# Stick-breaking attention by pairs of heads, with filler products and early output chunks

## Chip, cores and metric

One core of a Trainium2 chip runs the whole program. Its engines are TensorE (matrix products), VectorE, ScalarE and GpSimd, with SyncE for issuing transfers; each takes its own instructions in order and they meet through semaphores. The metric is the device time of one execution in microseconds (us).

## The reference

The program runs two transformer-like blocks of two layers each on 256 tokens of 1024 features, in float32. Only one sublayer bears on the change: stick-breaking attention, in the first layer of the second block, 16 heads of 64.

```python
def stick_breaking_attention(h, w_qkv, w_o):
    ...
    q = qkv[0] * (SB_HEAD_DIM ** -0.5)
    k, v = qkv[1], qkv[2]
    for blk in range(S // Q_BLOCK):
        ...
        z = jnp.einsum('bhqd,bhkd->bhqk', q[:, :, t0:L], k[:, :, :L])
        mask = s_idx[None, :] < t_idx[:, None]
        log_keep = jnp.where(mask, jax.nn.log_sigmoid(-z), 0.0)
        later = lax.cumsum(log_keep, axis=3, reverse=True) - log_keep
        w = jnp.where(mask, jnp.exp(jax.nn.log_sigmoid(z) + later), 0.0)
        outs.append(jnp.einsum('bhqk,bhkd->bhqd', w, v[:, :, :L]))
    ...
    return o @ w_o
```

With sp(z) = log(1 + e^z), which is -log_keep, a weight is exp(z - the sum of sp over this key and all later ones), and zero where the mask is off.

## The kernel before

The program is a list of stages (`plan`). Most are slab stages: a weight slab of 16 blocks of 128 x 128 arrives in `raw`, ScalarE rounds it to `w_hi` (L633), VectorE subtracts the rest into `w_lo` (L1166), and TensorE multiplies it with three products per block (`mm3`, L1911 to L1913: high by high, high by low, low by high). A slab has two halves f of 8 chunks k; slabs alternate between two places p. Beside them VectorE makes modulation products (L1194) from rows that GpSimd's queue loads.

The stage `stick` stands between the projections for q, k and v (L825 is the last copy of v) and the output projection (`out`, kind "b"). Keys lie on the partitions. A head has 384 columns of scores: 256 queries for the first 128 keys and 128 queries for the last 128 keys. For each head h, by step:

- TensorE: scores z into `pb[0][:, h % 2]` (L2315, L2316, float32, over 64 rows).
- ScalarE: w = ln(1 + exp(-|z|)) in three chained instructions (L1055 to L1057), read from PSUM.
- VectorE: zm = z + mask (0 or -1e30, L1792), w = max(z, 0) + w, which is sp(z) (L1794), and w times the 0/1 mask on the two outer thirds (L1797).
- TensorE, for head h - 2: products of w with a triangular table and with a table of -1, which give the negative sums over this and later keys, into `pb[1]` (L2324 to L2327).
- VectorE, for head h - 1: adds zm to them (L1801). ScalarE, for head h - 2: exp (L1061).
- TensorE, for head h - 4: products with v into half of the rows of `ps_o` (L2337 to L2339). ScalarE and VectorE then make the high and low part of the result in `e_hi`, `e_lo` (L1066, L1807).

`sb_z` in the arena has three turns of three 384-column buffers. In step h == 3 VectorE also makes the last two modulation products of the stage before. The output projection's first half slab waits for the low parts chunk by chunk (in `half`), f = 0 for all k, then f = 1.

Of the kernel before, what the change touches and what calls it, by code (L numbers as in the profile page):

```python
# [25 lines left out]
P = 128  # L26
# [50 lines left out]
TB = T + 2  # L77

# [67 lines left out]
def build(nc, a):  # L146
# [148 lines left out]
    with ExitStack() as ctx:  # L295
# [60 lines left out]
        sb_z = view(6144, 3, 3, 384)  # L356
# [5 lines left out]
        assert free0 + 4096 <= 11392 and 8320 + 2 * RC * P <= 11392 and 6144 + 3456 <= 11392  # L362
# [55 lines left out]
        def table(name):  # L418
# [37 lines left out]
        st_z, st_ln, st_sp, st_r, st_v, st_w, st_o, st_hi, st_lo = (  # L456
            sem(f"st_{k}") for k in ("z", "ln", "sp", "r", "v", "w", "o", "hi", "lo"))
# [158 lines left out]
        def _(act):  # L616
# [431 lines left out]
            def do_stick(n):  # L1048
                for h in range(SB_H + 4):
                    if h < SB_H:  # L1050
                        act.wait_ge(st_z, h + 1)
                        z, w = pb[0][:, h % 2, 0:384], sb_z[:, h % 3, 0, :]

                        wait_up(act, st_r, h - 2)
                        link(nc.scalar.activation(w, z, ACT.Abs))  # L1055
                        link(nc.scalar.activation(w, w, ACT.Exp, scale=-1.0))
                        nc.scalar.activation(w, w, ACT.Ln, bias=1.0).then_inc(st_ln, 1)  # L1057
                    if 2 <= h < SB_H + 2:
                        k = h - 2
                        act.wait_ge(st_v, k + 1)  # L1060
                        nc.scalar.activation(sb_z[:, k % 3, 2, :], sb_z[:, k % 3, 1, :], ACT.Exp).then_inc(st_w, 1)  # L1061
                    if h >= 4:
                        k = h - 4
                        r = HD * (k % 2)
                        act.wait_ge(st_o, k + 1)
                        nc.scalar.activation(e_hi[r:r + HD, k // 2, :], ps_o[r:r + HD, k % 2, 0:T],  # L1066
                                             ACT.Copy).then_inc(st_hi, 1)
# [81 lines left out]
        def _(dve):  # L1149
# [632 lines left out]
            def do_stick(n):  # L1782
                edges = lambda v: v.rearrange("p (b c) -> p b c", b=3)[:, 0:3:2, :]
                sv = next(s for what, s in plan if what == "slabs" and s.kind == "v" and s.arg["heads"] == SB_H)
                dve.wait_ge(masks_in, 16)
                for h in range(SB_H + 4):
                    if h < SB_H:
                        z, w, zm = pb[0][:, h % 2, 0:384], sb_z[:, h % 3, 0, :], sb_z[:, h % 3, 1, :]
                        dve.wait_ge(st_ln, h + 1)

                        wait_up(dve, st_w, h - 2)
                        nc.vector.tensor_tensor(zm, z, masks[:, 384:768], ALU.add).then_inc(st_sp, 1)  # L1792

                        nc.vector.scalar_tensor_tensor(out=w, in0=z, scalar=0.0, in1=w, op0=ALU.max, op1=ALU.add)\  # L1794
                            .then_inc(st_sp, 1)
                        dve.wait_ge(st_sp, 3 * h + 2)
                        nc.vector.tensor_tensor(edges(w), edges(w), edges(masks[:, 0:384]), ALU.mult).then_inc(st_sp, 1)  # L1797
                    if 1 <= h <= SB_H:
                        k = h - 1
                        dve.wait_ge(st_r, k + 1)  # L1800
                        nc.vector.tensor_tensor(sb_z[:, k % 3, 1, :], pb[1][:, k % 2, 0:384], sb_z[:, k % 3, 1, :],  # L1801
                                                ALU.add).then_inc(st_v, 1)
                    if h >= 4:
                        k = h - 4
                        r = HD * (k % 2)
                        dve.wait_ge(st_hi, k + 1)
                        nc.vector.tensor_tensor(e_lo[r:r + HD, k // 2, :], ps_o[r:r + HD, k % 2, 0:T],  # L1807
                                                e_hi[r:r + HD, k // 2, :].bitcast(F32), ALU.subtract)\
                            .then_inc(st_lo, 1)
                    if h == 3:  # L1810
                        mods(sv, sv.bodies - 1, 1, False, True)
# [92 lines left out]
        def _(pe):  # L1904
# [123 lines left out]
            def half(s, b, p, f, is_first):  # L2028
# [17 lines left out]
                else:  # L2046
                    xs = chunks(s, b, p, f)
                    n, one = len(xs), s.kind == "down"
                    for k, x in enumerate(xs):
                        if is_first and p == 0 and f == 0:  # L2050
# [3 lines left out]
                            if s.kind == "out" and s.arg["kind"] == "b":  # L2054

                                pe.wait_ge(st_lo, 2 * k + 2)
# [89 lines left out]

            def open_pair(i):
# [9 lines left out]
            def do_slabs(s):  # L2157
                def body(b, is_first, last):
                    for p in range(2):
# [14 lines left out]
                        elif s.kind == "merge" and is_first and p == 0:  # L2174
                            merge_first(s)
                        else:
# [127 lines left out]

            def do_stick(n):
                pe.wait_ge(tab_in, 16)
                pe.wait_ge(q_copied, n["had"]["q"])
                pe.wait_ge(v_copied, n["had"]["v"])
                for h in range(SB_H + 4):
                    if h < SB_H:  # L2310

                        wait_up(pe, st_sp, 3 * h - 4)
                        c, r = h // 2, HD * (h % 2)
                        q, k_ = dst["sbq"][r:r + HD, c, :], dst["sbk"][r:r + HD, c, :]
                        nc.tensor.matmul(pb[0][:, h % 2, 0:256], k_[:, 0:P], q, start=True, stop=True)  # L2315
                        nc.tensor.matmul(pb[0][:, h % 2, 256:384], k_[:, P:T], q[:, P:T], start=True, stop=True)\  # L2316
                            .then_inc(st_z, 1)
                    if 2 <= h < SB_H + 2:
# [192 lines left out]
```

## Time and profile before

| | |
|---|---|
| median of 3 runs | 2317.43 us (2315.99 to 2321.75) |
| span of the profiled execution | 2318.1 us |
| TensorE products busy | 2228.3 us (96%) |
| VectorE, ScalarE busy | 1837.1 us (79%), 1308.9 us (56%) |
| stick stage, first scores to first output product | 1546.2 to 1597.9 us |
| mean granted TensorE clock | 0.984 |

The profile is of one execution. Busy times of an engine are shares of that span; a wait is shown as idle time in front of an instruction with what released it. The granted clock is 1.00 at 2.4 GHz and 0.50 at 1.2 GHz.

### The profile page before, as it was taken

The page shows a single profiled execution, that of the slowest core. Times are in us where ns is not written, and L with a number is a line of the kernel's source. Part 1 is how long each engine was busy: PE and PEld are TensorE (multiplying, and loading weights), DVE is VectorE, ACT ScalarE, POOL GpSimd, SP SyncE. Part 2 cuts the span into 40 slices and gives each one's busy share as a digit, 9 for nine tenths or more (in the row PEclk, how much of TensorE's full clock was granted, in tenths as well). Part 3 has the DMA queues.
Part 4 walks back from the last instruction along what each step waited for, and adds up shares of the span by engine and source line. Part 5 has one row for each costly group of instructions (what it writes and reads, how often), then busy time and mean ns, then how long its engine had stood idle before and what let it go on. Part 6 is the DMA issues. An engine that isn't in the chain of part 4 may idle for free.

```text
span 2318.1 us, 49499 instructions
## 1 busy us (share of the span) xinstructions
PE 2228.3 (96%) x18082; PEld 2145.7 (93%) x18082; DVE 1837.1 (79%) x3245; ACT 1308.9 (56%) x2142; POOL 119.9 (5%) x231
## 2 busy tenths in 40 slices
PE   7899999999999999999999999999999999979998
PEld 5798899998899999889999999988999999979998
DVE  4886866799789988978998878768877877878655
ACT  4366655536776554576665644657544644686443
POOL 0100000000000100000000001010001001000000
PEclk8999999999999999999999999999999999999999
DMA  9745676765358765534778687662777677635654
GB/s 360 243 143 188 231 243 203 257 200 172 116 172 276 266 229 199 174 119 163 241 261 281 230 272 265 212 224 82 236 276 264 227 278 267 229 118 178 227 168 132
DMA packets 150550, 499.80 MB, mean 216 GB/s; under 512 B 17408, under 2 KB 21632, under 8 KB 148864
## 3 DMA queue, kind: packets, MB, share of 16 engines
q1 hardware_dynamic: 113504, 374.01, 47.0%
q0 software_dynamic: 32544, 119.55, 16.3%
q10 hardware_dynamic: 4352, 4.20, 0.6%
q8 instruction: 99, 1.62, 0.3%
q14 instruction: 51, 0.42, 0.1%
HBM read 496.65 MB, written 1.05 MB: 215 GB/s over the span
## 4 chain that ended last, share of the span: by engine, by line
PE 71%; DVE 15%; ACT 6%; DMA 4%; issue 3%; ACTq 0%; SPq 0%; DVEq 0%; POOLq 0%; POOL 0%
PE bank_pair L1911 22%; PE bank_pair L1913 21%; PE bank_pair L1912 21%; DVE w_lo L1166 4%; DVE arena L1452 2%; DMA modraw<-in_w_mod 2%; ACT w_hi L633 2%; PE bank_pair L2034 1%; PE ps_o L1924 1%; DVE h_lo L1328 1%; DVE small L1528 1%; ACT arena L873 1%; DVE arena L1725 1%; ACT h_hi L718 1%; DMA e_plain<-in_w_mod 0%
## 5 line engine op out<-in xcount | busy, mean ns | idle before, releaser
L1166 DVE TENSOR_TENSOR w_lo<-raw,w_hi 128x1024 fp32r<-128x1024 f32 (+2 forms) x748 | 820.9, 1113 | 198.9 <-ACT w_hi L633 195.1
L633 ACT ACTIVATE w_hi<-raw 128x1024 fp32r<-128x1024 f32 (+2 forms) x748 | 714.2, 967 | 406.8 <-PE bank_pair L1913 274.3
L1911 PE MATMUL bank_pair<-h_hi,w_hi 128*128 128x256 f32 x2928 | 841.8, 287 | 13.3 <-DVE arena L1725 5.8
L1912 PE MATMUL bank_pair<-h_lo,w_hi 128*128 128x256 f32 x2928 | 831.4, 284 | 0.0
L1913 PE MATMUL bank_pair<-h_hi,w_lo 128*128 128x256 f32 x2928 | 831.3, 284 | 0.0
L1911 PE MATMUL bank_pair<-e_both,w_hi 128*128 128x256 f32 (+1 forms) x2064 | 593.0, 287 | 19.0 <-DVE e_both L1846 10.0
L1911 PEld LDWEIGHTS bank_pair<-h_hi,w_hi 128*128 128x128 f32 x2928 | 564.8, 193 | 35.5 <-issue 25.0
L1912 PE MATMUL bank_pair<-e_both,w_hi 128*128 128x256 f32 (+1 forms) x2064 | 587.4, 285 | 0.0
L1913 PE MATMUL bank_pair<-e_both,w_lo 128*128 128x256 f32 (+1 forms) x2064 | 587.2, 285 | 0.0
L1912 PEld LDWEIGHTS bank_pair<-h_lo,w_hi 128*128 128x128 f32 x2928 | 565.1, 193 | 0.3
L1913 PEld LDWEIGHTS bank_pair<-h_hi,w_lo 128*128 128x128 f32 x2928 | 564.8, 193 | 0.0
L1911 PEld LDWEIGHTS bank_pair<-e_both,w_hi 128*128 128x128 f32 x2064 | 399.0, 193 | 26.9 <-issue 16.7
L1912 PEld LDWEIGHTS bank_pair<-e_both,w_hi 128*128 128x128 f32 x2064 | 399.4, 194 | 0.3
L1913 PEld LDWEIGHTS bank_pair<-e_both,w_lo 128*128 128x128 f32 x2064 | 399.1, 193 | 0.0
L1194 DVE SCALAR_TENSOR_TENSOR modraw<-modraw,cact 128x1024 f32<-128x1024 f32 x174 | 211.9, 1218 | 20.2 <-DMA modraw<-in_w_mod 19.8
L588 POOL DMA_DIRECT2D modraw<-in_w_mod x216 | 114.1, 529 | 1997.7 <-DVE modraw L1194 1657.9
L1452 DVE SCALAR_TENSOR_TENSOR arena<-arena,par 128x256 f32<-128x256 f32 x360 | 149.8, 478 | 4.0 <-PE bank_pair L2254 3.8
L1725 DVE SCALAR_TENSOR_TENSOR arena<-bank_pair,par,arena 128x255 f32<-128x255 f32 x240 | 99.3, 477 | 40.1 <-ACT arena L1007 39.0
L1038 ACT ACTIVATE arena<-bank_pair 128x256 f32<-128x256 f32 x80 | 30.7, 383 | 114.2 <-PE bank_pair L1913 114.2
L1005 ACT ACTIVATE arena<-bank_pair,par 128x256 f32<-128x256 f32 x60 | 33.8, 564 | 104.1 <-PE bank_pair L1913 104.1
L1634 DVE SCALAR_TENSOR_TENSOR x_res<-bank_pair,cols,x_res 128x256 f32<-128x256 f32 (+1 forms) x128 | 60.6, 481 | 27.2 <-PE bank_pair L1913 25.8
L1760 DVE TENSOR_TENSOR arena<-bank_pair,arena 128x256 f32<-128x256 f32 x80 | 33.9, 424 | 48.7 <-ACT arena L1038 48.7
(264 smaller groups left out, 2176.2 us busy)
## 6 DMA issues: line engine op xcount, KB each, us to landing
modraw<-in_w_mod POOLq DMA_DIRECT2D x216, 512.0 KB, 4.9
raw<-in_w_gu SPq DMA_DIRECT2D x176, 512.0 KB, 4.6
raw<-in_w_up SPq DMA_DIRECT2D x132, 512.0 KB, 5.1
raw<-in_w_gate SPq DMA_DIRECT2D x48, 512.0 KB, 3.7
raw<-in_w_dn SPq DMA_DIRECT2D x64, 384.0 KB, 4.3
raw<-in_w_dn SPq DMA_DIRECT2D x64, 320.0 KB, 3.5
raw<-in_w_down SPq DMA_DIRECT2D x48, 384.0 KB, 5.0
raw<-in_w_down SPq DMA_DIRECT2D x48, 320.0 KB, 4.4
```

The lines of the kernel that those rows point to most:

```text
L588: nc.gpsimd.dma_start(modraw[:, c, :], a["w_mod"][m, :, D * c:D * (c + 1)]).then_inc(mod_in[c], 16)
L633: nc.scalar.activation(w_hi[:, p, HALF * f:HALF * f + w], raw[:, p, HALF * f:HALF * f + w], ACT.Copy)\
L1005: nc.scalar.activation(scr[:, p, 0, :], z[:, 0, :], ACT.Identity, bias=fb[:, j, :], scale=taps[:, j, 1:2])
L1166: nc.vector.tensor_tensor(w_lo[:, p, at], raw[:, p, HALF * f:HALF * f + w], w_hi[:, p, at].bitcast(F32), ALU.subtract).then_inc(lo_ready, 1)
L1194: nc.vector.scalar_tensor_tensor(out=modraw[:, p, :], in0=modraw[:, p, :], scalar=1.0, in1=vector, op0=ALU.mult, op1=ALU.mult, accum_out=m ...
L1452: ins = nc.vector.scalar_tensor_tensor(out=o, in0=u, scalar=w[:, j, t:t + 1], in1=o, op0=ALU.mult, op1=ALU.add)
L1634: nc.vector.scalar_tensor_tensor(out=x[:, k, :], in0=pb[p][:, q, 0:T], scalar=cols[:, 2, :].unsqueeze(2)[:, k, :], in1=x[:, k, :], op0=ALU ...
L1725: nc.vector.scalar_tensor_tensor(out=o, in0=i_, scalar=taps[:, FC * q + j, 0:1] if left else taps[:, FC * q + j, 2:3], in1=o, op0=ALU.mult ...
L1760: ins = nc.vector.tensor_tensor(scr[:, p, 1, :], z[:, 1, 0:T], scr[:, p, 0, :], ALU.mult)
L1911: nc.tensor.matmul(out, l[0], r[0], start=start, stop=False)
L1912: nc.tensor.matmul(out, l[0], r[1], start=False, stop=False)
L1913: return nc.tensor.matmul(out, l[1], r[0], start=False, stop=stop)
```

## The change

Two heads (a pair, i = 0 to 7) are handled together.

- Each VectorE and ScalarE operation covers 2 x 384 columns. `sb_z` has three turns of two buffers of 768 columns; the closing exp writes over the first.
- The mask is added first, by VectorE from PSUM; ScalarE's abs, exp and ln then read the masked scores from the arena, and the multiplication with the 0/1 mask is gone. The tri-products take all 384 columns of a head in one product, and a second one adds the later keys' sums.
- Products of the two heads alternate: scores on rows 0 to 63 and 64 to 127, values on columns 0 to 63 and 64 to 127 of the array.
- In step i TensorE makes the scores of pair i, the tri-products of i - 1 and the values of i - 2. VectorE: mask addition i, max-and-add i - 1, addition i - 2, low part i - 3. ScalarE: abs, exp, ln of i, copy of i - 3, closing exp of i - 2.
- `keep_warm` adds 3 and 6 float32 products of 256 columns, whose results nobody reads, after the scores of pairs 0 and 1.
- Ahead of the values of the last pair TensorE makes chunks 0 to 4 of both halves of the first output slab (`out_early`); chunks 5 to 7 follow (`out_rest`), in the order k, f.
- The two modulation products go to step 9, between the last addition and the low part of pair 6.

```diff
             def do_stick(n):                         # ScalarE
+                for i in range(SB_P + 3):
+                    if i < SB_P:
+                        w, zm = sb_z[:, i % 3, 0], sb_z[:, i % 3, 1]
+                        act.wait_ge(st_zm, i + 1)
+                        wait_up(act, st_o, i - 2)
+                        link(nc.scalar.activation(w, zm, ACT.Abs))
                         link(nc.scalar.activation(w, w, ACT.Exp, scale=-1.0))
                         nc.scalar.activation(w, w, ACT.Ln, bias=1.0).then_inc(st_ln, 1)
+                    if i >= 3:
+                        k = i - 3
+                        act.wait_ge(st_o, k + 1)
+                        nc.scalar.activation(e_hi[:, k, :], ps_o[:, k % 2, 0:T], ACT.Copy).then_inc(st_hi, 1)
+                    if 2 <= i < SB_P + 2:
+                        k = i - 2
                         act.wait_ge(st_v, k + 1)
+                        nc.scalar.activation(sb_z[:, k % 3, 0], sb_z[:, k % 3, 1], ACT.Exp).then_inc(st_w, 1)
...
             def do_stick(n):                         # VectorE
+                for i in range(SB_P + 3):
+                    if i < SB_P:
+                        dve.wait_ge(st_z, i + 1)
+                        wait_up(dve, st_w, i - 2)
+                        nc.vector.tensor_tensor(sb_z[:, i % 3, 1], pb[0][:, :, 0:384], far, ALU.add).then_inc(st_zm, 1)
+                    if 1 <= i < SB_P + 1:
+                        k = i - 1
+                        w, zm = sb_z[:, k % 3, 0], sb_z[:, k % 3, 1]
+                        dve.wait_ge(st_ln, k + 1)
+                        nc.vector.scalar_tensor_tensor(out=w, in0=zm, scalar=0.0, in1=w, op0=ALU.max, op1=ALU.add)\
                             .then_inc(st_sp, 1)
+                    if 2 <= i < SB_P + 2:
+                        k = i - 2
                         dve.wait_ge(st_r, k + 1)
+                        nc.vector.tensor_tensor(sb_z[:, k % 3, 1], pb[1][:, :, 0:384], sb_z[:, k % 3, 1],
                                                 ALU.add).then_inc(st_v, 1)
+                    if i == SB_P + 1:
+                        mods(sv, sv.bodies - 1, 1, False, True)
+                    if i >= 3:
+                        k = i - 3
                         dve.wait_ge(st_hi, k + 1)
+                        nc.vector.tensor_tensor(e_lo[:, k, :], ps_o[:, k % 2, 0:T], e_hi[:, k, :].bitcast(F32),
+                                                ALU.subtract).then_inc(st_lo, 1)
...
+            def out_chunk(f, k):
+                pe.wait_ge(st_lo, k + 1)
+                c = HALF * f + P * k
+                return mm3(pb[0][:, f, 0:T], (w_hi[:, 0, c:c + P], w_lo[:, 0, c:c + P]),
+                           (e_hi[:, k, :], e_lo[:, k, :]), k == 0, k == DC - 1)
+            def out_early(s):
+                pe.wait_ge(lo_ready, 2 * s.l0 + 2)
+                pe.wait_ge(st_zm, SB_P)
+                for f in range(2):
+                    for k in range(SBO_EARLY):
+                        out_chunk(f, k)
+            def out_rest(s):
+                for k in range(SBO_EARLY, DC):
+                    for f in range(2):
+                        ins = out_chunk(f, k)
+                        if k == DC - 1:
+                            ins.then_inc(half_done, 1)
...
+            def keep_warm(n):
+                for _ in range(n):
+                    nc.tensor.matmul(ps_t[:, 0, 0:T], ones, table("cos"), start=True, stop=True)
...
             def do_stick(n):                         # TensorE
+                for i in range(SB_P + 2):
+                    if i < SB_P:
+                        wait_up(pe, st_zm, i)
+                        for keys, queries, at in ((slice(0, P), slice(0, T), slice(0, T)),
+                                                  (slice(P, T), slice(P, T), slice(T, T + P))):
+                            for hd in range(2):
+                                r = HD * hd
+                                ins = nc.tensor.matmul(pb[0][:, hd, at], dst["sbk"][r:r + HD, i, keys],
+                                                       dst["sbq"][r:r + HD, i, queries], start=True, stop=True)
+                        ins.then_inc(st_z, 1)
+                        if i < len(ST_WARM):
+                            keep_warm(ST_WARM[i])
+                    if 1 <= i < SB_P + 1:
+                        k = i - 1
+                        pe.wait_ge(st_sp, k + 1)
+                        wait_up(pe, st_v, k)
+                        for hd in range(2):
+                            w, o = sb_z[:, k % 3, 0, hd], pb[1][:, hd, :]
+                            nc.tensor.matmul(o[:, 0:384], table("ntri"), w, start=True, stop=False)
+                            ins = nc.tensor.matmul(o[:, P:T], table("nones"), w[:, T:T + P], start=False, stop=True)
+                        ins.then_inc(st_r, 1)
+                    if i >= 2:
+                        k = i - 2
+                        if k == SB_P - 1:
+                            out_early(so)
                         pe.wait_ge(st_w, k + 1)
                         wait_up(pe, st_lo, k - 1)
+                        for keys, queries, at in ((0, slice(0, T), slice(0, T)), (1, slice(T, T + P), slice(P, T))):
+                            for hd in range(2):
+                                v = dst["sbv"][:, keys, HD * (2 * k + hd):HD * (2 * k + hd + 1)]
+                                ins = nc.tensor.matmul(ps_o[HD * hd:HD * (hd + 1), k % 2, at], v,
+                                                       sb_z[:, k % 3, 0, hd, queries], start=keys == 0, stop=keys == 1)
+                        ins.then_inc(st_o, 1)
```

SB_P is 8 (pairs), SBO_EARLY is 5, ST_WARM is (3, 6).

## Rows read from the trace of the kernel before

**Rows 1.** The page's first line.
```profile
span 2318.1 us, 49499 instructions
```

**Rows 2.** Stretches: length, busy us of PE, PEld, DVE, ACT, POOL; clock, DMA, GB/s.
```profile
1547.13:1550.51 3.38, 0.00 (x0) 0.00 (x1) 3.35 (x7) 2.96 (x6) 0.53 (x1) 1.00 1.00 372
1551.30:1561.50 10.20, 10.20 (x39) 8.62 (x38) 5.63 (x13) 5.90 (x12) 0.00 (x0) 0.50 0.25 86
1561.60:1595.90 34.30, 34.12 (x229) 28.13 (x227) 30.35 (x66) 27.76 (x60) 1.05 (x2) 1.00 0.10 32
```

**Rows 3.** Time order of PE over one head: start us, us, engine, line, operands.
```profile
1586.41 0.70 PE L2315 MATMUL bank_pair<-arena 64*128 64x256 f32 x2
...
1587.26 0.49 PE L2324 MATMUL bank_pair<-arena,tab 128*128 128x128 f32 x2
...
1588.35 0.43 PE L2337 MATMUL ps_o<-arena 128*64 128x128 f32 x2
...
1589.14 0.48 PE L2315 MATMUL bank_pair<-arena 64*128 64x256 f32 x1
```

**Rows 4.** Time order of PE, one head's scores at half clock.
```profile
1553.39 1.22 PE L2315 MATMUL bank_pair<-arena 64*128 64x256 f32 x2
...
1554.97 0.79 PE L2324 MATMUL bank_pair<-arena,tab 128*128 128x128 f32 x2
```

**Rows 5.** Time order of PE in the first block's attention, scores of two heads.
```profile
983.62 1.13 PE L2254 MATMUL bank_pair<-arena 64*128 64x256 f32 x8
984.68 0.39 PE L1911 MATMUL bank_pair<-h_hi,w_hi 128*128 128x256 f32 x1
```

**Rows 6.** Time order: first scores and their reader; later, ScalarE's sequence.
```profile
1546.17 0.34 PEld L2315 LDWEIGHTS bank_pair<-arena 64*128 64x128 f32 x4 [0.95 <-issue]
...
1547.12 0.49 ACT L1055 ACTIVATE arena<-bank_pair 128x384 f32<-128x384 f32 x1 [1.07 <-PE bank_pair L2316]
...
1587.89 0.52 ACT L1056 ACTIVATE arena<-arena 128x384 f32<-128x384 f32 x1
...
1588.44 0.52 ACT L1057 ACTIVATE arena<-arena 128x384 f32<-128x384 f32 x1
...
1589.04 0.52 ACT L1061 ACTIVATE arena<-arena 128x384 f32<-128x384 f32 x1
...
1589.47 0.36 ACT L1066 ACTIVATE e_both<-ps_o 64x256 fp32r<-64x256 f32 x1
```

**Rows 7.** Groups of instructions by form: count, busy us, mean ns, idle before.
```profile
L1166 DVE TENSOR_TENSOR w_lo<-raw,w_hi 128x768 fp32r<-128x768 f32 x112 | 104.8, 955 | 23.4 <-ACT w_hi L633 23.1
L633 ACT ACTIVATE w_hi<-raw 128x768 fp32r<-128x768 f32 x112 | 93.5, 844 | 117.1 <-PE bank_pair L1913 63.8 <-DMA raw<-in_w_down 39.8 <-DMA raw<-in_w_dn 12.9
L1066 ACT ACTIVATE e_both<-ps_o 64x256 fp32r<-64x256 f32 x13 | 4.8, 371 | 0.3
L1194 DVE SCALAR_TENSOR_TENSOR modraw<-modraw,cact 128x1024 f32<-128x1024 f32 x174 | 211.9, 1218 | 20.2 <-DMA modraw<-in_w_mod 19.8
```

**Rows 8.** Time order of DVE, its first instruction in the stage.
```profile
1549.44 0.55 DVE L1792 TENSOR_TENSOR arena<-bank_pair,bias 128x384 f32<-128x384 f32 x1
```

**Rows 9.** Stretches of TensorE waits and of what came after two of them.
```profile
184.73:187.08 2.35, 0.00 (x1) 0.01 (x1) 2.25 (x7) 2.34 (x4) 0.00 (x0) 1.00 0.01 5
189.40:192.70 3.30, 3.30 (x18) 3.30 (x17) 1.33 (x4) 3.19 (x7) 0.00 (x0) 0.50 0.02 5
...
1293.61:1295.07 1.46, 0.00 (x1) 0.03 (x1) 1.33 (x2) 1.46 (x3) 0.00 (x0) 1.00 0.00 0
1295.10:1302.00 6.90, 6.83 (x55) 6.62 (x56) 6.90 (x14) 3.74 (x6) 0.00 (x0) 1.00 0.53 173
```

**Rows 10.** Time order of PE, the first output products.
```profile
1597.86 0.39 PE L1911 MATMUL bank_pair<-e_both,w_hi 128*128 128x256 f32 x1
...
1598.32 0.28 PE L1911 MATMUL bank_pair<-e_both,w_hi 128*128 128x256 f32 x1
...
1598.67 0.28 PE L1911 MATMUL bank_pair<-e_both,w_hi 128*128 128x256 f32 x1
```

More of the change, by code:

```diff
@@ L77 @@
 TB = T + 2
+SB_P = SB_H // 2
+SBO_EARLY = 5
+ST_WARM = (3, 6)
 F32 = mybir.dt.float32
@@ L361, in build @@
         l_i, l_t = e_plain[:, 0, RC:2 * RC, :], e_plain[:, 1, RC:2 * RC, :]
-        assert free0 + 4096 <= 11392 and 8320 + 2 * RC * P <= 11392 and 6144 + 3456 <= 11392
+        assert free0 + 4096 <= 11392 and 8320 + 2 * RC * P <= 11392 and 6144 + 4608 <= 11392
         mod_first = [e_plain[:, e, DC * k:DC * (k + 1), :].rearrange("p a b -> p (a b)")
@@ L1782, in do_stick @@
             def do_stick(n):
-                edges = lambda v: v.rearrange("p (b c) -> p b c", b=3)[:, 0:3:2, :]
                 sv = next(s for what, s in plan if what == "slabs" and s.kind == "v" and s.arg["heads"] == SB_H)
+                far = masks[:, 384:768].unsqueeze(1).broadcast_to([P, 2, 384])
                 dve.wait_ge(masks_in, 16)
[L1786 to L1794, printed above, removed]
+                for i in range(SB_P + 3):
[8 more added lines that the diff above has]
+                        nc.vector.scalar_tensor_tensor(out=w, in0=zm, scalar=0.0, in1=w, op0=ALU.max, op1=ALU.add)\
@@ L2175, in body @@
                             merge_first(s)
+                        elif s.kind == "out" and s.arg["kind"] == "b" and is_first and p == 0:
+                            out_rest(s)
                         else:
@@ L2303, in do_gate @@
                         ins.then_inc(att_o, 1)
+            def keep_warm(n):
+                for _ in range(n):
+                    nc.tensor.matmul(ps_t[:, 0, 0:T], ones, table("cos"), start=True, stop=True)
             def do_stick(n):
+                so = next(s for what, s in plan if what == "slabs" and s.kind == "out" and s.arg["kind"] == "b")
                 pe.wait_ge(tab_in, 16)
@@ L2308, in do_stick @@
                 pe.wait_ge(v_copied, n["had"]["v"])
[L2309 to L2318, printed above, removed]
-                        k = h - 2
-                        pe.wait_ge(st_sp, 3 * (k + 1))
-                        wait_up(pe, st_v, k - 1)
-                        w, o = sb_z[:, k % 3, 0, :], pb[1][:, k % 2, :]
-                        nc.tensor.matmul(o[:, 256:384], table("ntri"), w[:, 256:384], start=True, stop=True)
-                        nc.tensor.matmul(o[:, 0:128], table("ntri"), w[:, 0:128], start=True, stop=True)
-                        nc.tensor.matmul(o[:, 128:256], table("ntri"), w[:, 128:256], start=True, stop=False)
-                        nc.tensor.matmul(o[:, 128:256], table("nones"), w[:, 256:384], start=False, stop=True)\
-                            .then_inc(st_r, 1)
-                    if h >= 4:
-                        k = h - 4
-                        r = HD * (k % 2)
```

43 lines of the change are left out of this document (3 added, 40 removed).

## The prediction

> **What bounds the kernel now.** I read the page first, then a table of stretches around the stick-breaking stage, then the time order of each engine inside it. The stage and the first half slab of the output projection are all that the diff touches: from the first score product at 1546.2 to the output products that start at 1597.86 [rows 10]. Everything before runs as it did; what follows runs later or earlier as a block. So the question is only when the first output slab's p = 0 is finished. Its 48 products follow each other every 0.12 us (a chunk of L1911 to L1913 each) [rows 10], 5.76 us, so it is finished at 1603.6.
>
> Inside the stage TensorE is the bound. In the long middle it is busy 34.12 of 34.30 us at full clock, VectorE 30.35 and ScalarE 27.76 [rows 2]. One head takes from 1586.41 to 1589.14, 2.73 us, and the three groups of products stand back to back: scores 0.85, tri-products (L2324 on) 1.09, values 0.79 [rows 3]. At the start there is a hole: TensorE waits 3.38 us after the first two heads' scores [rows 2] because VectorE is still with weight splits and begins the first mask addition at 1549.44 [rows 8]; after it the granted clock is 0.50 (1.2 GHz) for 10.2 us, although TensorE is busy all of it [rows 2]. A group then lasts about twice as long: one head's scores 1.58 [rows 4].
>
> **Part by part.** *Columns.* A product of 256 columns in this type costs two passes of 0.213 us. A group costs its passes plus 0.2 us: the value group, 6 passes of 128 columns, took 0.79 [rows 3]. The total of columns of a pair is that of two heads. What changes is that neighbouring products of scores now use different halves of the array's rows, and those of values different halves of its columns. The attention of the first block does that already: eight passes of L2254 (four products of 256 columns) stand from 983.62 to 984.68, 1.06 us, where one after another they would need 1.71 plus 0.2 [rows 5]. So they run two at a time. A pair's scores cost 0.43 + 0.21 + 0.2 = 0.84 us and its values 0.79, where two heads took 1.69 and 1.58; the tri-products cost 1.71 + 0.2 = 1.91, where they took 2.18. TensorE's work for a pair falls from 5.46 to 3.54 us.
>
> *VectorE and ScalarE.* The 768-wide form costs 0.955 us on VectorE and 0.844 on ScalarE [rows 7]. For a pair VectorE has three of them and a low part, 3.3 us (before, eight passes, two edge masks and two low parts, over 4.8); ScalarE has four and a copy, 3.8. No engine's sum would hold the stage above 3.9 us for a pair, against 5.46 now. By the sums it gets faster.
>
> *The order.* The sums don't decide, because three things that were two steps apart are now one. In step i ScalarE does abs, exp and ln of pair i, then the copy of i-3, then the closing exp of pair i-2. TensorE puts the values of pair i-2, which wait for that exp, ahead of the scores of pair i+1, which feed the mask addition and with it ScalarE's next step. Before, the values in a step were those of four heads back, whose exp had been made two steps earlier, so nothing closed. Now it is a ring, with every link in it:
> abs and exp 2 x (0.844 + 0.03) = 1.75 [rows 7], where the 0.03 is what lies between 1587.89 and 1588.44 beyond 0.52 [rows 6]; ln, next instruction 0.09 before its end as L1066 after L1061 [rows 6], 0.75; copy 0.38 - 0.09 = 0.29 (the one head's copy took 0.371 [rows 7]); closing exp 0.844 and 0.04 of handing over, 0.88; values 0.79; scores from first weight load to the reader's start 0.95, as from 1546.17 to 1547.12 [rows 6]; mask addition 0.955 + 0.04 = 0.99. Sum 6.40 us for a pair, against 2 x 2.73 = 5.46. The tri-products lie beside it: they wait for the two VectorE operations of 0.87 each that follow the mask addition, start 1.73 after ScalarE's step and end 3.64 after it, and the closing exp ends 3.68 after it. So they are hidden with nothing to spare.
>
> *The start.* Mask addition of pair 0 at 1549.44 as before [rows 8], to 1550.4; ScalarE 1550.4 to 1553.0 (before, it had worked from PSUM ahead of VectorE, and now has to wait). Scores 1 at 1550.4, added by 1552.3; ScalarE on pair 1 to 1555.5; the max-and-add of pair 0 ends 1554.0, tri-products 0 to 1555.9; scores 2, addition to 1557.85. ScalarE's step of pair 2 begins at 1557.9. The fillers, 9 products of 0.43 us, fill 1547.0 to 1548.3 and 1551.3 to 1553.9, in front of nothing that is ready; at full clock they cost nothing. Should the clock be low there, six of them take 5.1 us instead of 2.6 in front of the first tri-products and cost about 3 us.
>
> *The middle and the end.* Five rings later, step 7 begins at 1557.9 + 5 x 6.40 = 1589.9. Then tri-products 6 done at 1593.6; their addition, behind the max-and-add of pair 7, to 1594.9; tri-products 7 1594.9 to 1596.9; values 6 to 1597.6. Output chunks 0 to 4 for both halves, 30 products of 0.12 = 3.6 us, to 1601.3: the closing exp of pair 7 is ready at 1598.9, so the early chunks hold up its values by 2.4 us, but they are work that has to be done. Values 7 to 1602.1; chunks 5 and 6 (1.44 us) cover copy and low part of pair 7 (0.38 + 0.43, done 1603.2); chunk 7 to 1604.4. The two modulation products (1.218 us each [rows 7]), moved from the middle to this end, delay the low part of pair 6 to 1600.7, needed at 1602.2: cost nothing; with less cover at most 2.4 us. POOL's next load of modulation rows starts some 35 us later with them, into a queue that is idle here; the next such product belongs to the next feed-forward block. SP's queue isn't touched: the weight slabs of the output were loaded before. The later splits wait for TensorE's half slab 0, which now ends together with half 1, 2.9 us later in the slab; a copy of 1.05 and a subtraction of 1.22 fit into the 5.76 us of p = 1.
> End of p = 0: 1604.4 against 1603.6, +0.8 us at full clock. The gain of the start (its 10.2 us at 1.2 GHz) and of the covered end is eaten by 0.94 us for each ring.
>
> *The clock.* In the ring TensorE works 3.54 us on end and then waits 2.86 us (some 2.6 by the profile's modelled ends). What do such waits do in this trace? After one of 2.35 us (184.73) the clock was 0.50 for the whole of 189.4 to 192.7; after one of 1.46 us (1293.61) it stayed at 1.00 [rows 9]; the one of 3.38 us was followed by 10.2 us at 0.50 [rows 2]. The trace has ten waits of TensorE of 1.9 us and more, these two among them, and each was followed by a fall; of seven between 1.2 and 1.7 us at most two were. Here one comes every 6.4 us and the only fillers are in the first two steps. A ring wholly at 1.2 GHz costs: values 1.48 and scores 1.74 instead of 0.79 and 0.95, +1.5, and the tri-products 3.7 instead of 1.91, which then end 1.77 after the closing exp, +1.8: 9.65 us, +3.25. Bounds: no ring hit, 0; all six hit, +19.5. After a fall the clock stayed low at least 3.3 us [rows 9], which is about the busy half of one ring, and the next wait may or may not be in full after it has risen; I take half of the rings, 3 x 3.25 = +9.8.
>
> The Trainium skill, "TensorE: Matmul & The Clock Gate", section "Why this matters for your kernels", warns only of idle gaps longer than the ring's wait. By that rule alone the clock would hold and the sum would be +0.8; this trace disagrees, with the fall after 2.35 us.
>
> **The sum.** +0.8 + 9.8 = +10.6 us. The profiled span is 2318.1 [rows 1], 0.7 above the median 2317.4 of three runs; the difference is set against the median: 2328.0 us.
>
> **Rivals.**
> 1. *Ring at full clock.* As above, but the waits, which here stand between stretches of full work, don't lower the clock: +0.8, between -1 and +4 (4 with a slow start that the fillers lengthen): 2318.2. For it: after 1.46 us the clock held. Against: the wait of 2.35 us [rows 9] is the nearer one to 2.6. It is also what the rule of the Trainium skill's "TensorE: Matmul & The Clock Gate" gives.
> 2. *Low clock in all rings.* +0.8 + 19.5: 2337.7. For it: the 10.2 us at 0.50 under full work in just this stage [rows 2]. Against: in a slowed ring TensorE works 6.9 of 9.65 us on end, and the 3.3 us at full work [rows 9] sufficed for a rise.
> 3. *Faster.* ScalarE's own sum bounds and the ring does not close: 3.85 for a pair. Its place is the values of pair i-2 ahead of scores i+1; were they an operation that is already released when TensorE comes to it, step 7 would begin at 1577.1 and p = 0 end 12.8 us earlier than with the ring: 2317.4 + 0.8 - 12.8 = 2305.4. It decides for faster by 0.3% once a ring is below 4.8 us. Against: each link is a semaphore in the diff; only shorter durations could do it, and the 768 forms are measured [rows 7].
>
> **Chances.** Forecast (cost of the clock 6 to 14 us, 2324.3 to 2332.3) 0.58; rival 1 0.24; rival 2 and what lies above the forecast 0.09; rival 3 0.09. The range has to take in the forecast and rival 1, 0.82: 2316.5 to 2335. A difference of 0.3%, 7 us, is about what a measurement can tell from none. Slower by more: the forecast but for its lowest corner and rival 2, 0.65; within: rival 1 and that corner, 0.26; faster 0.09.
>
> **What would show it.** In the profile after: the starts of the abs operations 6.4 us apart where the clock is 1.00 and up to 9.7 where it is 0.50; the closing exp of pair i-2 right after the copy that follows ln; TensorE idle some 2.6 us before each tri-group, released by VectorE's addition; two heads' scores within 0.84 us; several stretches at 0.50 between 1557 and 1600; output chunks 0 to 4 ahead of the last values without a wait. I am wrong if abs operations are under 5.5 us apart (a link is missing from the ring) or PEclk stays at 1.00 through the stage (rival 1).

## The result and the profile after

| | before | after |
|---|---|---|
| median | 2318.1 us (10 runs, 2314.3 to 2323.3) | 2325.4 us (10 runs, 2320.6 to 2333.2) |
| ratio | | 1.0027, 95% interval 1.0016 to 1.0039 |
| the same on another chip | 2318.6 us (9 runs) | 2328.5 us (5 runs), 1.0041 (1.0027 to 1.0055) |
| span of the profiled execution | 2318.1 us | 2324.5 us |
| stage, first scores to end of first output slab | 57.5 us | 67.1 us |

The change makes the kernel slower, by 6.3 us by the ratio. The forecast was 10.6 us.

The page of the changed kernel, its first line and the busy times:

```profile
span 2324.5 us, 49225 instructions
...
PE 2219.3 (95%) x18004; PEld 2130.5 (92%) x18004; DVE 1823.2 (78%) x3197; ACT 1298.5 (56%) x2102; POOL 119.9 (5%) x231
```

TensorE, VectorE and ScalarE all do less than before (2219.3 against 2228.3 us on TensorE), and the kernel takes longer. The page can't show more: a slice is 58 us, about the whole stage. The stretches from one abs operation to the next show it; columns as in rows 2. The first line is the start (scores 0 to step 2), the next five are one ring each, the last goes from step 7 to the end of the output slab:

```profile
1542.67:1553.69 11.02, 8.89 (x50) 6.64 (x50) 6.36 (x9) 4.95 (x6) 0.53 (x1) 1.00 0.62 226
1553.69:1562.97 9.28, 6.39 (x24) 3.95 (x24) 2.69 (x4) 3.26 (x5) 0.00 (x0) 0.63 0.00 0
1562.97:1571.14 8.17, 5.29 (x24) 3.43 (x24) 3.12 (x5) 3.53 (x6) 0.00 (x0) 0.79 0.01 2
1571.14:1577.65 6.51, 3.63 (x24) 2.45 (x24) 3.11 (x5) 3.53 (x6) 0.00 (x0) 1.00 0.00 0
1577.65:1586.90 9.25, 6.36 (x24) 3.94 (x24) 3.11 (x5) 3.53 (x6) 0.00 (x0) 0.63 0.00 1
1586.90:1595.05 8.15, 5.27 (x24) 3.41 (x24) 3.11 (x5) 3.53 (x6) 0.00 (x0) 0.79 0.00 0
1595.05:1609.79 14.74, 12.31 (x89) 9.93 (x89) 9.05 (x15) 7.31 (x12) 1.06 (x2) 1.00 0.21 63
```

Where TensorE was busy 34.12 of 34.30 us [rows 2], it is now busy 3.63 of 6.51, and VectorE and ScalarE about half of the time: no engine is the bound. The ring at full clock takes 6.51 us; with the same 12 products in it (24 passes, x24) it takes up to 9.28 where the mean clock is 0.63.

The ring itself, in the time order of ScalarE over that clean stretch (start, duration, line; idle time and releaser in brackets):

```profile
1571.14 0.84 ACT L1058 ACTIVATE arena<-arena 128x768 f32<-128x768 f32 x1 [4.57 <-DVE arena L1793]
1572.01 0.84 ACT L1059 ACTIVATE arena<-arena 128x768 f32<-128x768 f32 x1
1572.89 0.84 ACT L1060 ACTIVATE arena<-arena 128x768 f32<-128x768 f32 x1
1573.64 0.36 ACT L1064 ACTIVATE e_both<-ps_o 128x256 fp32r<-128x256 f32 x1
1573.90 0.83 ACT L1069 ACTIVATE arena<-arena 128x768 f32<-128x768 f32 x1
1577.65 0.84 ACT L1058 ACTIVATE arena<-arena 128x768 f32<-128x768 f32 x1 [2.92 <-DVE arena L1793]
```

The time order of TensorE beside it (L2357 and L2358 tri-products, L2370 values, L2345 scores):

```profile
1572.98 0.89 PE L2357 MATMUL bank_pair<-arena,tab 128*128 128x384 f32 x2 [2.88 <-DVE arena L1803]
...
1574.57 0.39 PE L2358 MATMUL bank_pair<-arena,tab 128*128 128x128 f32 x2
1574.88 0.87 PE L2370 MATMUL ps_o<-arena 128*64 128x256 f32 x8
1575.68 0.92 PE L2345 MATMUL bank_pair<-arena 64*128 64x256 f32 x8
1579.49 1.62 PE L2357 MATMUL bank_pair<-arena,tab 128*128 128x384 f32 x2 [2.88 <-DVE arena L1803]
```

And VectorE's mask addition (L1793), max-and-add (L1798), addition (L1803) and the next mask addition:

```profile
1570.14 0.96 DVE L1793 TENSOR_TENSOR arena<-bank_pair,bias 128x768 f32<-128x768 f32 x1 [3.86 <-PE bank_pair L2345]
1571.02 0.95 DVE L1798 SCALAR_TENSOR_TENSOR arena<-arena 128x768 f32<-128x768 f32 x1
1571.88 0.95 DVE L1803 TENSOR_TENSOR arena<-bank_pair,arena 128x768 f32<-128x768 f32 x1
...
1576.65 0.96 DVE L1793 TENSOR_TENSOR arena<-bank_pair,bias 128x768 f32<-128x768 f32 x1 [2.20 <-PE bank_pair L2345]
```

Two paths lead from one mask addition to the values, which stand ahead of the next scores.

- By way of VectorE and the tri-products, from start to start: mask addition 0.88, max-and-add 0.86, addition to the first tri-product 1.10, tri-products 1.90, values 0.80, scores to the next mask addition 0.97: 6.51. Each instruction on this path starts when the one before it hands over.
- By way of ScalarE: abs 0.87, exp 0.88, ln 0.75, copy 0.26, closing exp to the first value product 0.98, values 0.80, scores to mask addition 0.97, mask addition to the next abs 1.00: 6.51 as well, but with some room in it. Where TensorE does wait for the closing exp, in e4_all_later below, the values start 0.90 us after the start of that exp. Here it is 0.98, and the profile shows no wait of TensorE before the values: it was still at the tri-products.

So the tri-products' path sets the ring, and the one through ScalarE would give 6.43, only 0.08 us less. TensorE's two waits of 2.88 us have the same length; the product after the first lasts 0.89 us, after the second 1.62.

### The profile page after: what moved, and what is told of

It is laid out like the page before. It is cut to its first block, busy times and chain, and to the rows that moved or that the text cites. A ratio compares the mean times of both kernels' runs of the same rounds, so it can differ in the third digit from the quotient of the medians.

```text
span 2324.5 us, 49225 instructions
## 1 busy us (share of the span) xinstructions
PE 2219.3 (95%) x18004; PEld 2130.5 (92%) x18004; DVE 1823.2 (78%) x3197; ACT 1298.5 (56%) x2102; POOL 119.9 (5%) x231
## 3 DMA queue, kind: packets, MB, share of 16 engines
q8 instruction: 99, 1.62, 0.3%
## 4 chain that ended last, share of the span: by engine, by line
PE 71%; DVE 16%; ACT 7%; issue 4%; DMA 2%; ACTq 0%; SPq 0%; DVEq 0%; POOL 0%; POOLq 0%
PE bank_pair L1911 22%; PE bank_pair L1913 21%; PE bank_pair L1912 21%; DVE w_lo L1168 4%; DVE arena L1454 2%; ACT w_hi L636 2%; PE bank_pair L2034 1%; PE ps_o L1924 1%; DMA modraw<-in_w_mod 1%; DVE h_lo L1330 1%; DVE small L1530 1%; PE bank_pair L2357 1%; ACT arena L876 1%; DVE arena L1727 1%; ACT h_hi L721 1%
## 5 line engine op out<-in xcount | busy, mean ns | idle before, releaser
L1911 PE MATMUL bank_pair<-e_both,w_hi 128*128 128x256 f32 (+1 forms) x2064 | 592.2, 287 | 19.5 <-DVE e_both L1846 10.0
```

What stands on the lines that cost most here:

```text
L1911: nc.tensor.matmul(out, l[0], r[0], start=start, stop=False)
```

## The experiments

All start from the changed kernel unless said otherwise. "Stage" is the stretch from the first scores to the end of the first output slab in the profile.

### Filler products in every step

```diff
-ST_WARM = (3, 6)
+ST_WARM = (3, 6, 4, 4, 4, 4, 4, 4)
```

> Four filler products in each of the steps 2 to 7 as well, right after the scores; they take 1.7 of the 2.9 us that TensorE waits there. Theory (the ring costs 6.5 us a pair at full clock, and the low clock adds 8.9 us over five rings in the profile of after): the clock stays 1.00 through the stage, the abs operations stand 6.5 us apart in all rings, and the kernel is 6 to 10 us faster than the changed one, about 2316 to 2319, level with the kernel before. Rival (the low clock is beside the point, because the ring is bound by VectorE and ScalarE): no change from 2325. Rival (the fillers run into the tri-products): rings of 7 us or more, slower than 2325.

2320.6 us, 1.0005 of before (0.9992 to 1.0018); stage 58.8 us. The whole stage as one stretch:

```profile
1541.89:1600.66 58.77, 50.88 (x306) 37.54 (x307) 31.02 (x42) 29.65 (x42) 1.58 (x3) 1.00 0.18 60
```

The abs operations at both ends of one ring, in ScalarE's time order:

```profile
1559.88 0.84 ACT L1058 ACTIVATE arena<-arena 128x768 f32<-128x768 f32 x1 [3.18 <-DVE arena L1793]
...
1566.39 0.84 ACT L1058 ACTIVATE arena<-arena 128x768 f32<-128x768 f32 x1 [2.92 <-DVE arena L1793]
```

The clock is 1.00 throughout, all five rings take 6.51 us, and the end takes 14.74 us as before; only ScalarE's first abs came 3.95 us after the first scores and not 3.49. So the low clock accounts for 8.8 us of the first profile's stage (41.36 us for its five rings against 5 x 6.51). In the times the gain over the changed kernel is 4.8 us by the medians, less than the 6 to 10 expected: its first profile has four low stretches, and not every execution has as many (below). The interval just touches that of the first measurement of the changed kernel and is clear of the second's. Work that nobody reads makes the kernel faster here.

### No filler products

```diff
-ST_WARM = (3, 6)
+ST_WARM = ()
```

> The nine filler products of steps 0 and 1 are taken out. Theory: the clock falls in the first waits of the stage, rings 0 to 2 run partly at 1.2 GHz, where after they began only with the wait before tri-products 1; cost 0 to 3 us, because the fillers stand in front of nothing and later rings lose the clock either way: 2325 to 2328. Rival (the fillers delay real products): 1 to 3 us faster.

2329.3 us, 1.0043 (1.0027 to 1.0059); stage 67.6 us. The start, from the first scores to step 2:

```profile
1542.71:1557.15 14.44, 7.19 (x32) 4.88 (x32) 7.23 (x9) 5.06 (x7) 0.53 (x1) 0.65 0.47 154
```

14.44 us at a mean clock of 0.65, against 11.02 at 1.00. About half of the 3.4 us has nothing to do with the fillers: VectorE began its first mask addition 4.17 us after the first scores here and 2.51 us after them there. From the first abs to the third it is 9.29 us against 7.53, so the nine fillers are worth 1.8 us there. The five rings then lost 5.9 us to the low clock, less than the 8.8 of the first profile of the changed kernel. The time lies a little above the 2325 to 2328 expected, and the interval overlaps that of the changed kernel.

### Scores ahead of the values

```diff
-                for i in range(SB_P + 2):
+                for i in range(SB_P + 3):
                     ... scores of pair i
+                    if i >= 3:
+                        k = i - 3
+                        ... values of pair k
                     if 1 <= i < SB_P + 1:
                         k = i - 1
                         ... tri-products of pair k
-                    if i >= 2:
-                        k = i - 2
-                        ... values of pair k
```

> On TensorE only, the values of pair i-2 go behind the scores of pair i+1 instead of ahead of them. This cuts the ring found (abs, exp, ln, copy, closing exp, values, scores, mask addition); the next ring is mask addition, max-and-add, addition, tri-products, scores: 1.8 + 1.9 + 0.95 + 1.0, about 5.6 us a pair. Theory: abs operations 5.6 us apart at full clock, fewer falls of the clock because TensorE waits 2.0 us instead of 2.9; 6 to 12 us faster than after: 2313 to 2319. Rival (the spacing comes from the durations of the 768-wide operations and not from the order on TensorE): 6.5 us apart as before, 2325.

2320.5 us, 1.0009 (0.9999 to 1.0019); stage 58.8 us. TensorE's time order in one step:

```profile
1557.19 0.88 PE L2370 MATMUL bank_pair<-arena,tab 128*128 128x384 f32 x2 [2.88 <-DVE arena L1803]
...
1559.09 0.93 PE L2345 MATMUL bank_pair<-arena 64*128 64x256 f32 x8
1559.94 0.87 PE L2360 MATMUL ps_o<-arena 128*64 128x256 f32 x8
```

The abs operations of three steps, from ScalarE's:

```profile
1555.34 0.84 ACT L1058 ACTIVATE arena<-arena 128x768 f32<-128x768 f32 x1 [2.46 <-DVE arena L1793]
1561.05 0.84 ACT L1058 ACTIVATE arena<-arena 128x768 f32<-128x768 f32 x1 [2.38 <-DVE arena L1793]
1566.76 0.84 ACT L1058 ACTIVATE arena<-arena 128x768 f32<-128x768 f32 x1 [2.12 <-DVE arena L1793]
```

5.71 us from abs to abs at full clock, where 5.6 was expected: 6.51 less the 0.80 of the values. The move took them out of the ring; VectorE's three operations, the tri-products and the scores are what is left of it. No instruction of a pair has changed, only the order of two groups on TensorE; the rival that holds the 768-wide operations responsible is out. Two of the five rings still fell to a low clock (7.3 and 7.4 us), and the gain over the changed kernel, 4.9 us by the medians, is less than the 6 to 12 expected.

### Values and tri-products both one step later

Start: the experiment before.

```diff
                     ... scores of pair i
                     if i >= 3:
                         k = i - 3
                         ... values of pair k
-                    if 1 <= i < SB_P + 1:
-                        k = i - 1
+                    if 2 <= i < SB_P + 2:
+                        k = i - 2
                         ... tri-products of pair k
```

> As the experiment before, and the tri-products one step later too, at the end of TensorE's step: scores i, values i-3, tri-products i-2. The ring left is abs, exp, ln, copy, closing exp, mask addition: 2.6 + 0.3 + 0.9 + 0.99 - overlap, 4.7 us a pair; TensorE works 3.5 of it. Theory: abs 4.7 us apart, clock 1.00 in all of the middle, stage 17 to 19 us shorter than after, kernel 2306 to 2310, faster than before. Rival (ScalarE and VectorE slow each other or handing over costs more once all three run closely): above 5.5 us a pair, 2312 or more.

2313.2 us, 0.9972 (0.9961 to 0.9984): faster than the kernel before, though not the 2306 to 2310 expected. Two stretches, the middle and one of the last steps:

```profile
1559.00:1578.00 19.00, 14.72 (x101) 9.84 (x97) 12.91 (x17) 14.28 (x20) 0.00 (x0) 1.00 0.01 1
1583.50:1593.50 10.00, 8.08 (x27) 5.24 (x26) 1.71 (x3) 1.23 (x2) 0.00 (x0) 0.50 0.01 2
```

Three abs operations of the middle, in time order:

```profile
1564.06 0.84 ACT L1058 ACTIVATE arena<-arena 128x768 f32<-128x768 f32 x1 [1.09 <-DVE arena L1793]
1568.78 0.84 ACT L1058 ACTIVATE arena<-arena 128x768 f32<-128x768 f32 x1 [1.09 <-DVE arena L1793]
1573.51 0.85 ACT L1058 ACTIVATE arena<-arena 128x768 f32<-128x768 f32 x1 [1.09 <-DVE arena L1793]
```

Now TensorE waits for the closing exp, in each ring (ScalarE's exp, and the values from TensorE's time order):

```profile
1571.57 0.84 ACT L1069 ACTIVATE arena<-arena 128x768 f32<-128x768 f32 x1
...
1572.47 0.87 PE L2360 MATMUL ps_o<-arena 128*64 128x256 f32 x8 [1.07 <-ACT arena L1069]
```

Rings of 4.73 us, as expected (4.7), and the clock holds although TensorE waits 1.07 us in each. The missing 3 to 7 us are in the end, 21.7 us from the abs of pair 7 to the end of the slab against 14.74 in the changed kernel: after a wait of 1.93 us for the closing exp, 10 us at 0.50.

### The same with another order of the last steps

Start: the experiment before, its values and tri-products written as two functions. `out_early` leaves out the three chunks that `out_open` has made.

```diff
+OPEN = 3
...
+                    if i == SB_P:
+                        out_open(so)        # chunks 0 to 2 of half 0
-                    values(i)
-                    tris(i)
+                    for part in (tris, values) if i >= SB_P else (values, tris):
+                        part(i)
```

> As e4_all_later (rings of 4.7 us, but a stretch of 10.2 us at 1.2 GHz in its last steps), with the last steps in another order on TensorE: from step 8 on the tri-products stand ahead of the values, and three of the ten early output chunks go ahead of tri-products 6, into a wait. Theory (the low stretch follows TensorE's waits of 1.9 us there): no fall inside the stage, from the abs of pair 7 to the end of the first output slab 14 to 15.5 us instead of 21.7; 6 to 7 us faster than e4_all_later, about 2306 to 2308, the fastest of all. Rival (the tail is bound by the chain of additions and exps): under 3 us gained.

2308.2 us, 0.9961 (0.9946 to 0.9977), the fastest of all by its median and 9 us under the kernel before by the ratio. The stage:

```profile
1543.28:1590.50 47.22, 39.49 (x258) 28.81 (x259) 31.51 (x42) 29.72 (x42) 1.58 (x3) 1.00 0.20 69
```

47.2 us at full clock; from the abs of pair 7 to the end of the slab 14.5 us (14 to 15.5 expected, 21.7 in the kernel it starts from). The times moved by 5.0 us by the medians and 2.6 by the ratios, less than the 6 to 7 expected, and their intervals overlap: the tail's gain is clear in the profile and not in the times.

### Fillers in the kernel before

Start: the kernel before.

```diff
                             .then_inc(st_z, 1)
+                        if h == 1:
+                            for _ in range(7):
+                                nc.tensor.matmul(ps_t[:, 0, 0:T], ones, table("cos"), start=True, stop=True)
```

> The kernel before with seven filler products (3.0 us) after the scores of its second head, where TensorE waits 3.4 us in the profile. It measures what the fall of the clock at the start cost the kernel before. Theory (TensorE is the bound of its middle, and a head takes 3.58 us instead of 2.73 while the clock is low): 3 to 5 us faster than before, about 2314. Rival (the fall is made up for, since the steps after it are bound by VectorE catching up): no change. If it is 4 us faster, the change bought from its fillers what before could have had without pairs.

2312.4 us, 0.9973 (0.9961 to 0.9985); stage 53.8 us:

```profile
1542.21:1595.99 53.78, 52.19 (x350) 44.06 (x351) 45.18 (x91) 39.73 (x82) 1.58 (x3) 1.00 0.21 71
```

Six us of the median, from one added loop: as much as the reordered pairs of e4_all_later gave. The fall at the start of the stage was the kernel's own loss, and it had nothing to do with heads or pairs. The stage is 3.7 to 5.2 us shorter than in the three profiles of the kernel before (two of them below), 4.4 in the mean; where the other 2 us of the gain come from is not shown.

This gives the comparison at full clock in both kernels: 53.8 us before, 58.8 with pairs and fillers in every step. Clock aside, the change costs the stage 5.0 us. In the first profiles the low clock added 3.7 us to the stage before and 8.4 to the one after, which makes up the 9.6 us between 57.5 and 67.1.

### No early output chunks

```diff
-SBO_EARLY = 5
+SBO_EARLY = 0
```

> The changed kernel without output chunks ahead of the last pair (none early, all eight after it, order k then f). Theory: TensorE has work in the wait before the last values only because of them; without them the last values start 2.9 us sooner, and the 30 products come after, so the first output slab ends 0.7 to 3 us later: 2326 to 2329. Rival (early chunks delay the last values for nothing): equal or faster.

2328.1 us, 1.0034 (1.0024 to 1.0045). The stretch from the abs of pair 7 to the end of the slab:

```profile
1598.29:1614.50 16.21, 12.19 (x88) 9.95 (x89) 9.58 (x15) 7.31 (x12) 1.06 (x2) 1.00 0.28 77
```

TensorE's last value products with the wait ahead of them:

```profile
1607.86 0.87 PE L2370 MATMUL ps_o<-arena 128*64 128x256 f32 x8 [1.59 <-ACT arena L1069]
```

16.21 us against 14.74 with the chunks, both at full clock: they are worth 1.5 us. In the times the difference isn't resolved. The whole stage took 68.0 us in this profile. At its start the fillers did not hold the clock: VectorE came to the first mask addition 3.3 us after the first scores, and TensorE waited behind its three fillers:

```profile
1550.82 1.54 PE L2345 MATMUL bank_pair<-arena 64*128 64x256 f32 x8 [1.90 <-DVE arena L1793]
1552.29 3.88 PE L2330 MATMUL ps_t<-tab 128*128 128x256 f32 x12
```

The next six fillers (x12) took 3.88 us, against 2.86 in the changed kernel's first profile, in front of tri-products that were due, and from the first abs to the third it was 9.00 us, not 7.53.

### The modulation products back in step 3

```diff
-                    if i == SB_P + 1:
+                    if i == 3:
                         mods(sv, sv.bodies - 1, 1, False, True)
```

> The changed kernel with the two modulation products on VectorE back in step 3, as in the kernel before, instead of step 9. Theory: VectorE has waits of 3.9 us in each ring and of nothing behind it at the end, so both places are free: within 1 us of the changed kernel, 2325. Rival (in step 3 they stand in front of the low part of pair 0 and the next mask addition): one ring 1 to 2 us longer.

2329.2 us, 1.0041 (1.0026 to 1.0056), stage 64.0 us in its profile. The ring with the two products in it (POOL's two loads follow them) and the end of the stage without them, as stretches:

```profile
1566.32:1572.84 6.52, 3.63 (x24) 2.46 (x24) 5.32 (x9) 3.54 (x6) 1.06 (x2) 1.00 0.26 75
1596.84:1611.58 14.74, 12.31 (x89) 9.93 (x90) 6.87 (x11) 7.31 (x12) 0.00 (x0) 1.00 0.00 1
```

6.52 and 14.74 us, against 6.51 and 14.74 in the changed kernel: in this profile the products are free in either place, as expected, and the rival of a ring longer by 1 to 2 us is out. The stage is shorter than in the changed kernel's first profile because its rings lost 6.0 us to the clock and not 8.8. The times, 3.8 us longer by the medians with intervals that overlap, don't show a difference of the place.

### The two kernels again

Unchanged, for how far one profile speaks for all.

> The kernel before, unchanged, profiled a second time. In its first profile the stage (first scores to the end of the first output slab) took 57.5 us with one low stretch of 10.2 us. The filler in the kernel before gained 6 us in the times but only 3.7 us in the stage of its profile. Theory (the first profile shows a favourable position of the low clock; the usual stage is longer): 59 to 62 us here. Rival (the gain lies elsewhere in the kernel): 57.5 again.

> The kernel before, unchanged, a third profile. Theory: stage 59 to 62 us in most profiles. Rival: 57.5 within 0.5.

> The changed kernel, unchanged, profiled a second time; stage 67.1 us in the first profile with falls in three of five rings. Theory (where the falls lie differs from one execution to the next, and so do the rings of 6.5 and of 8 to 9.3 us): 63 to 69 us, abs operations 6.5 us apart where the clock is full.

> The changed kernel, unchanged, a third profile and five rounds on another chip. Theory: slower than before by 0.2 to 0.4%, as in the first measurement; stage 63 to 69 us. Rival (the first measurement was high by chance): within 0.15% of before.

The stage in the second profile of the kernel before:

```profile
1548.54:1606.54 58.00, 54.70 (x337) 46.10 (x338) 44.06 (x89) 40.38 (x82) 1.58 (x3) 0.88 0.20 68
```

in its third:

```profile
1547.08:1606.04 58.96, 54.92 (x337) 46.25 (x338) 45.34 (x91) 40.36 (x82) 1.59 (x3) 0.88 0.22 75
```

in the second of the changed kernel:

```profile
1541.49:1604.03 62.54, 43.78 (x259) 31.34 (x260) 30.36 (x42) 29.66 (x42) 1.59 (x3) 0.92 0.15 52
```

and in its third:

```profile
1542.72:1609.98 67.26, 48.31 (x258) 33.89 (x259) 30.52 (x42) 29.64 (x42) 1.58 (x3) 0.85 0.15 52
```

Before: 57.5, 58.0 and 59.0 us, mean 58.2; the second is below the 59 to 62 expected and the third at its bottom. After: 67.1, 62.5 and 67.3, mean 65.6, where 63 to 69 was expected; in the short one three rings of 6.51 us stand before the first fall. The difference of the means, 7.5 us, lies between what the two measurements of the times give by their ratios, 6.3 and 9.5. The times of e12_after_again came out 0.41% over before, a little beyond the upper end expected.

## Why the prediction was right, and where it was off

- **The ring.** Right that it closes, and where: the values ahead of the next scores. Predicted 6.40 us, measured 6.51 at full clock. Shown by taking the order apart: 5.71 us with one link moved, 4.73 with two. Which of its two paths is the later one was wrong, by little: the tri-products were to end 3.64 us after ScalarE's step begins and the closing exp 3.68, "hidden with nothing to spare". Measured, the tri-products let the values start after 3.74 us; the closing exp would have after 3.66 (0.87 + 0.88 + 0.75 + 0.26, and the 0.90 of e4_all_later). That is where the 0.10 us between the closing exp and the values comes from (0.88 taken, 0.98 measured). At 1.2 GHz the prediction itself has the tri-products end last.
- **The start.** Predicted 11.7 us from the first scores to step 2, measured 11.02. VectorE reached the mask addition 2.51 us after the scores and not 3.24: its last modulation product, for whose rows it waited in both profiles, began 0.92 us before the first scores here and 0.18 before them there. Over the profiles of the pair kernels shown here it is 2.2 to 4.2 us. All after that took what the sum said. The case that the prediction named, a low clock among the fillers at about 3 us, came up in the profile of e7_no_early and cost 1.5.
- **The pairs of products.** Right: eight passes of scores in 0.92 us by the modelled ends, values after 0.80.
- **The end.** Predicted 14.5 us from step 7, measured 14.74. The early chunks do hold the last values back, as said, by 2.1 us (11.69 us after the abs of pair 7, against 9.57 in e7_no_early); the experiment puts their worth at 1.5 us, for which the prediction had no price of its own.
- **The clock.** The term with the widest bounds, 0 to 19.5 us, taken as 9.8. Measured, five rings took 41.36 us against 5 x 6.51 = 32.55, so 8.8. In three profiles the loss was 8.8, 4.5 and 9.0 us (five rings less 32.55), 7.4 in the mean. The sum had counted six rings where five lie in the middle, and taken half of them as hit in full, 3.25 us each; in the first profile four were hit in part, the worst by 2.8. That 9.8 came so near to 8.8 is luck. The bounds were sound: all three profiles lie well between none and all. TensorE's wait was 2.88 us, not 2.6, and waits of this one length are followed by a fall in some rings and not in others; the prediction had gone by ten of ten followed by a fall, in one profile.
- **The stage and the kernel.** Predicted stage 57.4 + 10.6 = 68.0 us, measured 67.1. The spans differ by 6.4 only, since the changed kernel's first scores came 3.5 us earlier (1542.67 against 1546.20) in code that is the same in both: the first profile shows falls of the clock near 609, 688 and 1060 us that the second hasn't. With three profiles of each the stages differ by 7.5, so 10.6 was too large by 3: the changed stage is 65.6 in the mean and not 68.0, which is the clock term (7.4 and not 9.8), and the kernel before had been compared by its shortest stage, 57.5 where the mean is 58.2. The chance for "slower by over 0.3%" was set on it; the first measurement, 0.27%, is just inside "the same" by that bound, the second, 0.41%, outside.
- **The rivals.** The ring at full clock gives 58.8 us for the stage with fillers in every step, 1.3 over the first profile of before: that rival's price (+0.8) was near and its condition was not met. The rule of the Trainium skill on which it leaned (page "TensorE: Matmul & The Clock Gate", section "Why this matters for your kernels", long idle gaps only) does not agree with this case's traces: a fall followed waits of 2.88 us and, in e4_all_later, of 1.93 us. The rival of a low clock in all rings: none of three profiles. The faster rival named the point from which it would decide, a ring under 4.8 us at full clock: at 4.73 the kernel was faster by 0.28%, with a stretch of 10 us at low clock in it.
- **Small readings.** VectorE has six passes for two heads in the kernel before, not eight (mask addition, max-and-add and addition for each); its sum, over 4.8 us, is right. The trace of before has eight waits of TensorE between 1.2 and 1.7 us, not seven. Neither enters the forecast.

## What to carry to other kernels

When steps of several engines are pipelined by hand, write down for each instruction what stands ahead of it in its own queue, and look for a ring that closes within one step. Where two paths run beside each other, read from the waits which of them ends last: TensorE showed no wait for ScalarE's closing exp, so ScalarE's path wasn't the ring, though it came within 0.08 us of it. Here less work on every engine made the stage longer, and moving two groups on TensorE by one step took 1.8 us out of each of its rounds without touching an operation. TensorE, working in bursts, lost its clock to its own waits, so the ring was paid for twice, in a stage 5.0 us longer at full clock and in 8.8 us of low clock in the first profile; filler products are a quick test for that, and in the kernel before they alone gave as much as the pairs did once their steps were loosened (e4_all_later).

## What was not expected of the hardware

- Waits of the same length don't always cost the clock. In one profile, between the same instructions, 2.88 us of waiting (up to 1572.98) was followed by 1.00 over the ring and 2.88 us (up to 1579.49) by 0.63. The waits of 1.07 us in the rings of 4.73 were never followed by a fall; the first wait of 1.93 us in the same kernel was. Outside the stage, waits of 1.91 and 2.88 us (up to 606.43 and 685.72) kept the clock in the changed kernel's first profile, where the same two (1.90 and 2.88 us, up to 607.26 and 686.57) cost it in the one of before. What decides it is not shown.
- A copy of 256 columns from PSUM took 0.36 us of ScalarE on 128 partitions (1573.64), as much as on 64 in the kernel before (0.371 us in the mean), and the next activation started 0.10 us before its end.
